# Three mixers of a second model's layers: 64-row products, one decay array per level, heads by pairs, no GpSimd

## The reference, cut to what matters

```
mLSTM:     q, k = silu(causal_conv4(mq, mk));  D = b_t - b_s + i_s, masked causal
           S = (q k^T / 8) * exp(D - m);  h = (S v) / max(|sum S|, exp(-m));  y = sigmoid(o) * rms(h)
attention: 4 heads of 2 x 64: q, k = rope(rms(.) * gain);  p_c = softmax(mask(q_c k_c^T / 8)), c = 0, 1
           y = rms((p_0 - lambda * p_1) v)
HGRN2:     q = silu(.), k = (1-lb) sigmoid(-f), B = cumsum(log f)
           A[t,s] = sum_k q[t,k] k[s,k] exp(B[t,k] - B[s,k]), s <= t;  y = rms(A v) * silu(g)
```

## Time and profile before

| | us |
|---|---|
| median of 3 runs (2523.18 to 2529.94) | 2526.64 |
| the profiled execution | 2525.36 |
| its span | 2523.5 |
| mixers of the second model's first layer, 1691.8 to 1869.8 | 178.0 |
| mixers of its second layer, 2122.5 to 2300.0 | 177.5 |

### The profile page before, as it was taken

The page is one execution under the profiler, slowest core; times in us unless marked ns, Lnnn a source line. Parts: engine busy times, 40 slices in busy tenths (PEclk is TensorE's granted clock), DMA queues, the critical chain, the costliest instruction groups (busy, mean ns, idle before and its releaser), DMA issues.

```text
span 2523.5 us, 38956 instructions
## 1 busy us (share of the span) xinstructions
PE 2319.6 (92%) x16274; PEld 2151.5 (85%) x16274; DVE 1649.6 (65%) x2385; ACT 1375.4 (55%) x1936; POOL 50.0 (2%) x32
## 2 busy tenths in 40 slices
PE   7989999999999899998999999998678999867999
PEld 6979998999989799996888887787568999756999
DVE  4665546665566665555878888767766656785665
ACT  5755445544566453635777776755344445534443
POOL 0000000000000000000000000001000000110000
PEclk9989999999999999988999999998889999888999
DMA  6531334556554122334888888733114554202454
GB/s 224 160 99 51 106 104 146 170 173 186 157 163 159 59 71 97 126 113 159 305 306 297 312 312 298 268 126 124 42 43 142 194 187 156 95 25 75 144 193 140
DMA packets 111207, 398.14 MB, mean 158 GB/s; under 512 B 12336, under 2 KB 12336, under 8 KB 110768
## 3 DMA queue, kind: packets, MB, share of 16 engines
q1 hardware_dynamic: 111024, 395.58, 47.6%
HBM read 394.48 MB, written 1.05 MB: 157 GB/s over the span
## 4 chain that ended last, share of the span: by engine, by line
PE 65%; DVE 18%; ACT 10%; DMA 5%; issue 2%; SPq 0%; DVEq 0%; ACTq 0%
PE ps L390 64%; DVE wlo L1960 6%; DMA raw<-stream 4%; ACT whi L1183 4%; DVE arena L1960 3%; ACT arena L1193 2%; DVE arena L1968 1%; DVE h L1960 1%; DVE scr L1960 1%; ACT scr L1193 1%; ACT arena_r L1193 1%; ACT rst L1193 1%; DVE arena L1964 1%; DVE ul L1968 1%; DMA CO<-const 1%
## 5 line engine op out<-in xcount | busy, mean ns | idle before, releaser
L1960 DVE TENSOR_TENSOR wlo<-raw,whi 128x1024 fp32r<-128x1024 f32 (+1 forms) x762 | 909.6, 1207 | 539.1 <-ACT whi L1183 528.5
L1183 ACT ACTIVATE whi<-raw 128x1024 fp32r<-128x1024 f32 (+1 forms) x762 | 780.9, 1035 | 360.6 <-PE ps L390 288.3
L390 PE MATMUL ps<-uh,whi 128*128 128x256 f32 x2240 | 657.5, 294 | 20.8 <-DVE ul L1968 8.3
L390 PE MATMUL ps<-ul,whi 128*128 128x256 f32 x2240 | 638.4, 285 | 0.0
L390 PE MATMUL ps<-uh,wlo 128*128 128x256 f32 x2240 | 638.0, 285 | 0.0
L390 PE MATMUL ps<-arena_r,whi 128*128 128x256 f32 x2720 | 495.9, 285 | 26.1 <-DVE arena_r L1960 16.7
L390 PEld LDWEIGHTS ps<-uh,whi 128*128 128x128 f32 x2240 | 432.8, 193 | 34.0 <-issue 19.8
L390 PEld LDWEIGHTS ps<-arena_r,whi 128*128 128x128 f32 x2720 | 424.4, 192 | 31.2 <-issue 14.6
L390 PEld LDWEIGHTS ps<-ul,whi 128*128 128x128 f32 x2240 | 432.9, 193 | 7.0 <-issue 6.3
L390 PEld LDWEIGHTS ps<-uh,wlo 128*128 128x128 f32 x2240 | 432.7, 193 | 0.0
L390 PE MATMUL ps<-arena_r,wlo 128*128 128x256 f32 x1360 | 384.3, 283 | 0.0
(11 more groups left out here) (173 smaller groups left out, 1986.5 us busy)
## 6 DMA issues: line engine op xcount, KB each, us to landing
raw<-stream SPq DMA_DIRECT2D x694, 512.0 KB, 4.0
raw<-stream SPq DMA_DIRECT2D x64, 384.0 KB, 4.1
CO<-const SPq DMA_DIRECT2D x1, 2305.0 KB, 13.6
h<-xT SPq DMA_DIRECT2D x1, 1024.0 KB, 6.3
raw<-stream SPq DMA_DIRECT2D x4, 256.0 KB, 2.6
out<-h SPq DMA_DIRECT2D x4, 256.0 KB, 2.2
arena<-pT SPq DMA_DIRECT2D x2, 256.0 KB, 3.7
SM<-small SPq DMA_DIRECT2D x1, 464.0 KB, 3.3
```

Source lines behind the costliest of these rows:

```text
L390: return self.e.matmul(o, l, r, start=start, stop=stop, skip_group_check=True)
L1183: self.e.activation(M.whi[:, b:b + n], M.raw[:, a:a + n], ACT.Copy).then_inc(K.sem("weight_hi"), 1)
L1960: return self.e.tensor_tensor(o, a, b, op)
```

## The change

The projections, the eight levels, the weights and their split are the same. Around them:

1. Products over 64 channels use rows 0 to 63 or 64 to 127 of TensorE and of the operands, in place of 128 rows with half of the keys zeroed. The zeroed copies (`kz`, `akz`, `hkz`) go. Two heads of a pair write two banks.
2. One array of decays per level: ACT takes `Abs` of the difference, then `Exp` with scale -1. DVE multiplies queries and keys by it in one 128 x 1024 instruction. The mask write takes only the half of the columns that the level can touch.
3. Attention's mask is added by a product with the identity into the same bank; DVE takes the maximum and ACT the exponential straight from PSUM. mLSTM's mask (`late`, 0 or -1e30) is the third operand of the instruction that writes the exponents.
4. Heads go by pairs in one step: attention's heads 0 and 1, then 2 and 3; mLSTM's end once; one `group_norm` per two tiles, and the high and low parts of each pair right behind it. `w_out_2` waits tile by tile.
5. The rotary product and the sum of squares run together between the pieces; the root is multiplied in last, the gain in the copy. The convolution takes its taps from PSUM (six instructions per pair of tiles), `Silu` replaces sigmoid and product. mLSTM's thread starts four rounds later.
6. GpSimd keeps only two memsets.

```diff
+MLSTM = 4
 def mlstm(self, l):                              # on TensorE, DVE and ACT
+        for _ in range(MLSTM):
+            yield
...
+        for h in (0, 2):
+            two = [self.bank(work, "ms", l, h + z) for z in range(2)]
+            for z in range(2):
+                r = slice(64 * z, 64 * z + 64)
+                self.mm(two[z][:, 0:256], mqk[r, 2 + h // 2, 0:P], mqk[r, h // 2, :], True, True)
...
 def attention(self, l):                          # TensorE
+        def normed(n):
+            self.mm(b, M.co("rota"), B[which][:, t * T:(t + 2) * T], True, True)
+            self.mm(b, M.co("bones"), M.scr(K.slot("asq", which, l, t)), True, True)
+        for n, _ in enumerate(pieces):
+            if n % 2 and n > 1:
+                normed(n // 2 - 1)
+            yield
...
+                for z in range(2):
+                    for c in range(2):
+                        r = slice(64 * c, 64 * c + 64)
+                        self.mm(two[c][:, z * nk:(z + 1) * nk], aq[r, h + z, qt * P:(qt + 1) * P], ak[r, h + z, 0:nk],
+                                z == 0, False)
+                for c in range(2):
+                    self.mm(two[c][:, 0:2 * nk].rearrange("p (z n) -> p z n", z=2)[:, :, qt * P:nk], M.ident,
+                            wide(negm, P, 2), False, True)
...
 def level_scores(self, work, s, l, lev, q, k):
+        for h in range(4):
+            r = slice(64 * (h % 2), 64 * (h % 2) + 64)
+            for j in range(2):
+                last = self.mm(two[h % 2][:, at:at + P], k[r, h // 2, tk], q[r, h // 2, tq], True, True)
...
 def decays(lev):                                 # ACT
-            self.act(ke, ke, ACT.Exp).then_inc(*s("hke", l, lev))
-            self.act(dd, dd, ACT.Exp).then_inc(*s("hdd", l, lev))
+            self.act(E, E, ACT.Abs).then_inc(*s())
+            self.act(E, E, ACT.Exp, scale=-1.0).then_inc(*s("hE", l, lev))
...
 def hgrn(self, l):                               # DVE
-            self.ts(ke, dd, -1.0, MUL, 0.0, MIN).then_inc(*s("hke0", l, lev))
-            self.ts(dd, dd, 0.0, MIN).then_inc(*s("hdd0", l, lev))
+            self.tt(v3(x, 512), v3(B["hqk"], 512), wide(E, 512, 2), MUL).then_inc(*s("hqk", l, lev))
-                self.e.copy_predicated(ST[:, :, c0:c0 + P], mask, b)
+                    q = e.copy_predicated(later(d, lev), M.meet(lev), later(b, lev))
...
 def group_norm(self, s, l, t0, n, gain, times=None, *after):
+        q = self.stt(d, d, gain, self.rst("frs", l, t0)[:, 0:n * T], MUL, MUL)
...
+        for k in range(t0, t0 + n):
+            self.wait_ge(*self.K.when("mixh", l, t0))
+            self.tt(self.M.mixp[1][:, k, :], mix[:, k * T:(k + 1) * T], self.M.mixp[0][:, k, :].bitcast(F32), SUB)
...
 class Pool, layer_b
-        self.e.tensor_tensor(E, E, wide(M.co("causal"), 384, 4), MUL).then_inc(*s("mE2", l))
-        for lev in range(8):
-            self.e.tensor_tensor(dd, dd, B["hq"], MUL).then_inc(*s("hgq", l, lev))
```

More of the change, by code:

```diff
@@ L1 @@
 from contextlib import ExitStack, nullcontext
-from itertools import accumulate
+from itertools import accumulate, chain
 import numpy as np
@@ L236, in weave, with together @@
                 live.remove(th)
+def together(threads):
+    live = list(threads)
+    while live:
+        live = [th for th in live if next(th, "end") != "end"]
+        if live:
+            yield
 def beside(thread, other, k):
@@ L1023, in mlstm @@
[L1023 to L1031, removed]
+            last = self.apply_T(b[:, pt * T:(pt + 1) * T], lambda j, h: halves[:, h % 2, :], E, two)
@@ new lines, in mlstm @@
+        last.then_inc(*s("ps", "md", l))
+        b = self.bank(work, "me", l)
+        x = M.scr(K.slot("mden", l))
+        self.wait_ge(*K.when("mpick", l))
+        for pt in range(2):
+            last = self.mm(b[:, pt * T:(pt + 1) * T], x[0:4, pt * P:(pt + 1) * P], rN, True, True)
+        last.then_inc(*s("ps", "me", l))
+        b = self.bank(work, "mn", l)
+        for t in range(2):
+            self.wait_ge(*K.when("mv", l, t))
+        for pt in range(2):
+            last = self.apply_T(b[:, pt * T:(pt + 1) * T], lambda j, h: mv[:, j, h, :], E, [2 * pt, 2 * pt + 1])
@@ L1033, in attention @@
+        last.then_inc(*s("ps", "mn", l))
+        yield
+        yield from self.group_norm(work, s, l, 0, 2, M.co("bones"))
     def attention(self, l):
@@ L1036, in attention @@
         yield
[L1037 to L1049, removed]
@@ L1110, in hgrn @@
             yield
[L1111 to L1120, removed]
+            self.wait_ge(*K.when("hqk", l, lev))
+            x = B["QK"][:, lev % 2 * 1024:lev % 2 * 1024 + 1024]
+            q, k = v3(x[:, 0:512]), v3(x[:, 512:1024])
+            self.level_scores(work, s, l, lev, q, k)
             yield
@@ L1838, in attention @@
         for h in (0, 2):
-            pair = [head(h), head(h + 1)]
-            while pair:
-                for x in list(pair):
-                    if next(x, "end") == "end":
-                        pair.remove(x)
-                    yield
+            yield from heads(h)
     def hgrn(self, l):
@@ L1887, in hgrn @@
             yield
+            if lev == 7:
+                for z in range(2):
+                    self.wait_ge(*K.when("ps", "hs", l, 7, z))
+                    self.act(v3(B["ST"][:, z * 1024:(z + 1) * 1024], 512)[:, :, P:T],
+                             v3(self.bank("hs", l, 7, z))[:, :, 0:P], ACT.Copy).then_inc(
+                        *s(("hst", l, z), ("free", "hs", l, 7, z)))
             yield
```

617 lines of the change are left out of this document (275 added, 342 removed).

## The result

| | before | after |
|---|---|---|
| median, us | 2527.39 (four runs, 2523.18 to 2529.94) | 2488.95 (four runs, 2488.69 to 2491.82) |
| ratio, 95% interval | | 0.9852 [0.9835, 0.9869] |
| profiled execution, us | 2525.36 | 2488.69 |
| forecast, us | | 2485, range 2458 to 2514 |

A forecast was written before the change was run, and what follows sets the result against it. A chain alternating TensorE, DVE, ACT and GpSimd bounds two stretches. Per layer, 11 us early plus 106.3 shrinking to 89.6 gives 27.3, less 6 for clock: 21, 42 in all; 2526.6 - 42 = 2485 us, range 2458 to 2514.

The forecast's parts named there:

- DVE's work: Cross-check on the stretches: some 37 of 132 us of DVE go per layer, no gain by itself.
- Up to the first level: Stretch start to the first level's products: they end at 1752.9 instead of 1763.5, gain 11 us.
- Next rounds: Rounds 10 to 18 after the first level: 13.6, 12.8 and 20.9 us; rounds 19 to 32: 34.9 us.
- forty-seven as today: Rounds 10 to 18: 47.3 us, as before (48), now with attention's first pair entirely in it.
- rival 2: Mixer stretches: long attention steps make levels wait, 13 us per layer lost; gain 16, 2511 us; chance 22%.
- The clock: TensorE prices are warm but these windows run at 0.75 to 0.88: about 6 us more per layer.
- Tail: Last level to `w_out_2`: 7.4 us where 28.8 stood; the four joining copies leave the path.
- Halves side by side: 64-row products on two row halves: no overlap or half the time, 8 us of path per layer; taken as 0.
- rival 1: Levels and scores: row halves run side by side on TensorE, gain 42 + 16 = 58, 2469 us; chance 20%.
- Mode changes: TensorE switching between 64 and 128 rows, about 30 per layer: 0.16 us each, 5 per layer; taken as 0.
- rival 3: Levels and denominator: `Abs` loads tables, 23 us of ACT per layer, 2531 us; 8% including similar slower mishaps.
- Rival 4: Before the first level: DMA or splits hold the pieces; 17 needed in 61 us; rejected, no chance given.

## Why the prediction was right, step by step

**What bounded it** held: the two stretches carry the gain, and one chain over three engines makes them. Outside them the first layer is unchanged (15.5 of 15.6 lie ahead of `w_out_2`).

**DVE's work.** 37 us a layer forecast, 35.9 measured. Its most uncertain term, GpSimd's time beside DVE, was forecast at 10 a layer from one split, and the run that gave GpSimd's work to DVE puts it at about 9 (17.8 for two, an estimate). Put back into the changed kernel the same work costs DVE only 3.5 a layer (6.9 for two), yet 11.3 us of time. I take it that the stalls meet splits and products that the levels stand behind; no run shows which.

**Up to the first level** I forecast 1752.9; its products end at 1749.4. The reason was right (pieces run through, root and convolution lie beside them); the 17 pieces were right, and the wait of 2 for HGRN2's keys isn't there. The first window's 56.14 of 57.30 says it. Undoing root last takes back 6.3 of the 15.0 us gained there, and 16 in all.

**Next rounds.** By round groups in the first layer (each ends with a level's mask write), forecast and measured: 10 to 12, 13.6 and 20.3; 13 to 15, 12.8 and 12.5; 16 to 18, 20.9 and 26.0; 19 to 23, 14.3 and 13.4; 24 to 26, 13.3 and 15.7; 27 to 32, 7.3 and 8.1. Two groups carry the miss of the step "forty-seven as today".

- Rounds 10 to 12: I counted TensorE's chain and left DVE out, which has no pause from 1746.95 to 1763.7. In DVE's timeline the first level's mask write stands behind a split, a turned pair and the convolution's taps:

```profile
1746.95 2.36 DVE L1998 TENSOR_TENSOR wlo<-raw,whi 128x1024 fp32r<-128x1024 f32 x2 [2.31 <-ACT whi L1224]
...
1753.02 2.42 DVE L2006 SCALAR_TENSOR_TENSOR arena<-ps,SM,arena 128x255 f32<-128x255 f32 x6
1755.36 1.28 DVE L2858 COPY_PREDICATED arena<-CO,ps 128x256 f32<-128x256 uint8 x2
...
1766.28 1.23 DVE L1998 TENSOR_TENSOR wlo<-raw,whi 128x1024 fp32r<-128x1024 f32 x1 [2.50 <-ACT whi L1224]
```

and ACT has the split of a piece behind mLSTM's exponentials, so DVE's low part, and attention's maximum behind that, wait for them:

```profile
1762.50 2.79 ACT L1234 ACTIVATE arena<-arena 128x512 f32<-128x512 f32 x3 [3.74 <-DVE arena L1998]
1765.20 1.04 ACT L1224 ACTIVATE whi<-raw 128x1024 fp32r<-128x1024 f32 x1
...
1793.50 1.29 ACT L1234 ACTIVATE arena<-arena 128x512 f32<-128x512 f32 x2 [8.46 <-DVE arena L1998]
1794.70 0.61 ACT L1234 ACTIVATE scr<-arena 128x512 f32<-128x512 f32 x1
1795.22 0.58 ACT L1234 ACTIVATE arena<-ps 128x512 f32<-128x512 f32 x1
```

- Rounds 16 to 18: the last three rows are the next level's Abs and Exp and mLSTM's square in front of attention's copy; the output products wait 3.46 for it (1795.94), and what follows runs cold: 2.90 for these four products (eight records), 2.07 for a sum that I priced at 1.0 and that the warm clock does in 1.02, 3.09 for a level and the four 64-row products beside it. This is rival 2, "held by the order", in part: it would have cost 13 a layer, and the middle missed the forecast by 7.7. It isn't repaired by moving single threads. Longer gaps between attention's steps show the hold most clearly, since the levels come 12.8 earlier, but attention then ends last (+10). A later end of mLSTM (0) and other orders (+13, +24) don't help either.

**The clock.** I set 6 us a layer aside for it. The middle ran at 0.77 and 0.73, lower than the 0.83 and 0.85 before: with its projections moved ahead TensorE is idle more, and I read the lower clock as a consequence of the change (idle 30.4 of these 95.7 us before, 35.0 after); no run tested it. A price from warm rows was too low for rounds 16 to 18 above all. How much of the middle's miss is clock and how much is order, no run separates.

**Tail.** 7.4 forecast, 9.9 measured, with the four joining copies gone as said. What I hadn't counted is the clock behind it, in the second layer: of its 21.9, 4.3 come after `w_out_2` has begun. Before, nine groups of its products ran at 0.64 there behind a wait of 3.71. With the 4 a layer gained ahead of the first level it made up most of what the middle lost (7.7 a layer), so the total is nearer to its forecast than its parts are to theirs. At the marks of `w_out_2` the layers gain 15.5 and 17.6, 33 of the 42; that the total missed by only 4 is in part luck.

**Costs that no row showed.** Halves side by side: they overlap, 2.02 to 1.26 a level, with no effect on the time, so rival 1's mechanism is real and its gain of 16 is not. Its price stood on 8 us of path per layer; grouping by halves, 0.45 longer in each level, cost nothing that shows. Mode changes: a level's 64-row products last 1.26 and the 4-row product behind them starts 1.19 after their start, with no idle time at the change, as far as ends that the profile models can show it: the value taken, 0. So the drain that the Trainium skill names ("TensorEngine Tiling (Array Packing)", Key Properties) is not seen here, while its parallel tiles are. Mask writes with gaps take 0.38 each, and even full ones cost nothing that shows. `Abs`: `1793.50 1.29 ... x2` is Abs and Exp of 512 columns each, with no load between; rival 3 falls. The Trainium skill, "ScalarE: Activation LUTs", Table sets, had it so, and the trace agrees. The change does add two table loads of 1.28 a layer that I hadn't priced (ten in the stretch, eight before), none of them between Abs and Exp. Rival 4 fell with the first window.

**What would show it.** GpSimd has two memsets a layer, DVE 96.9 in the stretch (95 to 100), the tail 9.9 (under 12), the first level at 1749.4, rounds 10 to 26 take 87.9 (under 90). `w_out_2` near 1849 was wrong by 6 (1855.1), and the level products take 1.26 when warm, a sign by which I had said I would be wrong: it is a sign about their length, not about the path.

**Parts don't add up.** Undoing GpSimd, root, tile-wise waiting, spread steps and delay costs 11, 16, 13, 10 and 7, 57 in all, of a gain of 38. Each is the price of a delay in the changed kernel, not its share of the gain.

## What to carry to other kernels

When hand-woven threads share in-order engines, count for every round the work on each engine that stands in front of the one instruction the next engine waits for, not only the chain of the busiest engine; 36 us of work a layer left DVE here and the first layer got 15.6 shorter, and longer mask writes cost nothing that shows. Take work out of the places where TensorE would stop, and start the next large product on whatever part of its input is ready: the half clock behind a pause of 4.5 us cost 2.6 more. Price what stands behind a pause with cold rows.

## What the runs showed of the hardware

- Products that use rows 0 to 63 and 64 to 127 in turn, with different PSUM banks, overlap: eight float32 products of 128 columns take 2.02 us on 128 rows, 1.71 grouped by half, 1.26 in pairs, 1.16 alternating one by one.
- A wait of 4.50 us left TensorE at half clock for 5.8 us of work (0.64 for three products in place of 0.355). A wait of 1.96 (`1857.31`) did not in the changed kernel: the products behind it run at 0.355 a group. But the wait alone doesn't decide it. With attention's steps spread, a wait of 1.94 at the same place (`1856.23`) was followed, from 1857.4 to 1860.9, by products at 0.64 a group, at a granted clock of 0.51:

```profile
1857.97 0.63 PE L413 MATMUL ps<-arena_r,whi 128*128 128x256 f32 x2
```

- A DVE split of 1.23 takes 3.73 beside a GpSimd instruction of 3.48 that reads SBUF; over the run it is 0.2 us for each us of GpSimd in the changed kernel, and about 0.6 (an estimate) in the kernel before.
